# Low weights that are loaded as stationary operands, 32 bytes off the 128-byte phase of the other buffers

## The reference

```
x += 0.5 * SwiGLU_1(RMSNorm(x))                  # 1024 -> 2816 (gate and up) -> 1024
x += W_out [ DiffAttn | ConformerConv | ShortGatedConv ](W_in RMSNorm(x))
x += CrossAttn(RMSNorm(x), RMSNorm(mem))         # 4 heads of 256, 256 memory tokens
x += 0.5 * SwiGLU_2(RMSNorm(x))
```

## Time and profile before

| | |
|---|---|
| three runs, median | 1149.59 us |
| the same, lowest | 1149.45 us |
| the profiled execution's own time | 1149.58 us |
| its span, first to last instruction | 1147.8 us |
| mean granted TensorE clock | 1.00 of 2.4 GHz |
| PE busy | 1140.2 us, 99% of the span |
| DVE busy, ACT busy | 851.1 us (74%), 653.4 us (57%) |

### The profile page before, as it was taken

One profiled execution on the slowest core, in us unless ns is written; L12 is line 12 of the kernel. 1 busy time (PEld: TensorE's weight loads), 2 busy tenths in 40 slices (PEclk: granted clock), 3 DMA queues, 4 the chain that ended last, 5 costly groups with the idle time before them and its releaser, 6 DMA issues.

```text
span 1147.8 us, 15676 instructions
## 1 busy us (share of the span) xinstructions
PE 1140.2 (99%) x6180; PEld 985.8 (86%) x6180; DVE 851.1 (74%) x1164; ACT 653.4 (57%) x937; POOL 21.6 (2%) x63
## 2 busy tenths in 40 slices
PE   9999999999999999999999999999999999999997
PEld 8888888888889888888888888888888888888886
DVE  7767667899967676666786676669998676766756
ACT  6555556547755564545565554565577556645444
POOL 1000000000000000000000000000000000000000
PEclk9999999999999999999999999999999999999999
DMA  8865645644444366555546655544545443656551
GB/s 284 316 207 171 206 157 180 220 148 170 166 167 158 113 224 204 181 190 195 191 152 244 202 183 193 193 162 168 184 147 209 158 147 128 220 175 208 173 191 61
DMA packets 66265, 210.92 MB, mean 184 GB/s; under 512 B 5008, under 2 KB 24208, under 8 KB 61072
## 3 DMA queue, kind: packets, MB, share of 16 engines
q1 hardware_dynamic: 65216, 209.26, 53.6%
q10 hardware_dynamic: 976, 0.66, 0.2%
HBM read 208.85 MB, written 1.05 MB: 183 GB/s over the span
## 4 chain that ended last, share of the span: by engine, by line
PE 95%; DVE 4%; DVEq 1%; issue 0%; ACT 0%
PE G L1663 28%; PE G L1667 15%; PE D L1531 10%; PE D L1532 10%; PE D L1533 10%; PE G L1624 3%; PE D L1624 3%; PE G L1531 3%; PE G L1533 3%; PE G L1532 3%; PE G L1630 2%; DVE w_lo L974 1%; PE D L1630 1%; DVE acc L1181 1%; PE D L1598 1%; DVEq L1183 1%
## 5 line engine op out<-in xcount | busy, mean ns | idle before, releaser
L974 DVE TENSOR_TENSOR w_lo<-w_raw,w_hi 128x2048 fp32r<-128x2048 f32 (+3 forms) x260 | 452.2, 1746 | 54.8 <-ACT w_hi L563 53.8
L563 ACT ACTIVATE w_hi<-w_raw 128x2048 fp32r<-128x2048 f32 (+3 forms) x260 | 381.6, 1476 | 39.5 <-PE D L1533 16.9
L1663 PE MATMUL G<-a,w_hi 128*128 128x512 f32 x1406 | 339.7, 390 | 0.0
L1663 PEld LDWEIGHTS G<-a,w_hi 128*128 128x128 f32 x1406 | 260.8, 188 | 52.7 <-issue 0.9
L1667 PEld LDWEIGHTS G<-a,w_lo 128*128 128x128 f32 x1406 | 184.2, 191 | 9.5
L1667 PE MATMUL G<-a,w_lo 128*128 128x256 f32 x1406 | 187.0, 282 | 0.0
L1078 DVE TENSOR_TENSOR zqk<-G,zqk 128x512 f32<-128x512 f32 x88 | 60.7, 690 | 153.5 <-ACT zqk L642 153.2
L642 ACT ACTIVATE zqk<-G 128x512 f32<-128x512 f32 x88 | 52.4, 595 | 180.8 <-PE G L1667 180.5
L1531 PE MATMUL D<-w_hi,hT_hi 128*128 128x512 f32 x352 | 138.2, 393 | 0.0
L1532 PE MATMUL D<-w_lo,hT_hi 128*128 128x512 f32 x352 | 137.9, 392 | 0.0
L1533 PE MATMUL D<-w_hi,hT_lo 128*128 128x512 f32 x352 | 137.0, 389 | 0.0
(11 more groups left out here) (261 smaller groups left out, 1270.1 us busy)
## 6 DMA issues: line engine op xcount, KB each, us to landing
w_raw<-w_dram SPq DMA_DIRECT2D x120, 1024.0 KB, 5.0
w_raw<-w_dram SPq DMA_DIRECT2D x143, 512.0 KB, 5.4
m_raw<-memT_dram SPq DMA_DIRECT2D x2, 1024.0 KB, 9.4
w_raw<-w_dram SPq DMA_DIRECT2D x6, 256.0 KB, 5.8
w_raw<-w_dram SPq DMA_DIRECT2D x8, 128.0 KB, 4.0
vx<-mem_dram SPq DMA_DIRECT2D x1, 1024.0 KB, 10.7
x<-x_dram SPq DMA_DIRECT2D x2, 256.0 KB, 4.9
gbc<-fin_dram SPq DMA_DIRECT2D x1, 512.0 KB, 7.6
```

The costliest lines, as they stand in the source:

```text
L563: A(w_hi[:, part(i)], w_raw[:, part(i)], ACT.Copy).then_inc(s_hi, 1)
L974: V.tensor_tensor(w_lo[:, part(i)], w_raw[:, part(i)], w_hi[:, part(i)].bitcast(F32), ALU.subtract).then_inc(s_lo, 1)
L1663: M(banks[b], whi[:, at:at + P], both, start=k == 0, stop=False)
```

## The change

`w_lo` gets 192 more columns, and each block a place of its own in it, `PLACE_LO`. A block's columns are moved on by 32 columns (128 bytes) for each 1024 columns that lie before it, which leaves its phase, and the blocks whose low part is stationary in products of 256 columns by 8 columns (32 bytes) more. These are the 107 `gu` blocks of the feed-forward parts, the queries' 12 blocks, the 8 blocks of the memory's keys, and blocks 6, 7 and 8 of `in`, 133 of the 261. (In block 6 of `in` the low part moves; the change gives it the 32 bytes too.) All other blocks keep phase 0. `w_raw` and `w_hi` stay as they are. The buffers behind `w_lo` move on by 768 bytes, a multiple of 128, so their phase stays.

No instruction is added, removed or moved on any engine: each engine's list is that of before, row by row, apart from line numbers (31 more near the end of the file) and from the addresses that it reads and writes.

```
+LINE = 32
+SHIFT = 8
+GROUP = 1024
+RING_LO = RING + LINE * (RING // GROUP)
+
+def lo_is_stationary(name):
+
+    stage, piece = name[1], name[2]
+    if stage in ("ffn1", "ffn2"):
+        return piece[0] == "gu"
+    return stage == "q" or (stage == "kv" and piece < 4) or (stage == "in" and piece in (6, 7, 8))
+
+def lo_places():
+
+    place = []
+    for i, (name, w) in enumerate(RING_BLOCKS):
+        place.append(PLACE[i] + LINE * (PLACE[i] // GROUP) + (SHIFT if lo_is_stationary(name) else 0))
...
-        w_lo = sb("w_lo", [P, RING], F32R)
+        w_lo = sb("w_lo", [P, RING_LO], F32R)
...
+        def part_lo(i):
+
+            return slice(PLACE_LO[i], PLACE_LO[i] + RING_BLOCKS[i][1])
...
-                V.tensor_tensor(w_lo[:, part(i)], w_raw[:, part(i)], w_hi[:, part(i)].bitcast(F32), ALU.subtract
+                V.tensor_tensor(w_lo[:, part_lo(i)], w_raw[:, part(i)], w_hi[:, part(i)].bitcast(F32), ALU.subtract
...
-                return w_hi[:, part(i)], w_lo[:, part(i)]
+                return w_hi[:, part(i)], w_lo[:, part_lo(i)]
```

More of the change, by code:

```diff
@@ L102 @@
 PLACE, BEFORE = ring_places()
+LINE = 32
[11 more added lines that the diff above has]
+        place.append(PLACE[i] + LINE * (PLACE[i] // GROUP) + (SHIFT if lo_is_stationary(name) else 0))
+        for j in range(i):
+            apart = PLACE[j] + RING_BLOCKS[j][1] <= PLACE[i] or PLACE[i] + w <= PLACE[j]
+            assert not apart or place[j] + RING_BLOCKS[j][1] <= place[i] or place[i] + w <= place[j]
+    return place
+PLACE_LO = lo_places()
 TRANSFERS = [2 if (name[1] == "q" and name[2] >= 4) or (name[1] == "in" and name[2] in (7, 8)) or (
@@ L1014, in first_norm @@
                 dve.drain()
-                V.tensor_tensor(w_lo[:, part(0)], w_raw[:, part(0)], w_hi[:, part(0)].bitcast(F32), ALU.subtract
+                V.tensor_tensor(w_lo[:, part_lo(0)], w_raw[:, part(0)], w_hi[:, part(0)].bitcast(F32), ALU.subtract
                                 ).then_inc(s_lo, 1)
@@ L1671, in first_gate_up @@
             def first_gate_up():
-                whi, wlo = w_hi[:, part(0)], w_lo[:, part(0)]
+                whi, wlo = w_hi[:, part(0)], w_lo[:, part_lo(0)]
                 pe.wait_ge(s_first_w, 1)
```

## The result

The changed kernel takes **1152.79 us** (median of 9 runs, 1152.37 to 1153.27) against 1149.59 us before. The ratio is 1.0028 with a 95% interval of 1.0018 to 1.0039: slower by 0.3%, 3.2 us, where 0.45% faster was forecast, and outside the range of 1138.8 to 1150.4. Both forecast and result lie within the 2% about which the prediction gives 0.98.

The account below looks back on a forecast made before the run. PE's own steps were taken to bound the kernel. The only counted term, 5.2 us from 1726 low products at 3 ns each, gave 1149.6 - 5.2 = 1144.4 us, 0.45% faster; range 1138.8 to 1150.4.

Parts of the forecast that it names:

- What bounds the kernel: Whole kernel: PE is busy 1140.2 of 1147.8 us and waits 1.3 us, so the time is the sum of PE's steps.
- DVE's writes off phase: The 260 subtractions of line 974 write 32 bytes further on; cost nothing, since even a tenth more leaves DVE below PE.
- The larger margins of DVE and ACT: In a feed-forward piece of 8.28 us, DVE has 2.8 us and ACT 4.1 us to spare.
- The shifted low parts, stationary: 1726 products of lines 1667 and 1630 that load shifted low weights gain 3 ns each, 5.2 us.
- Products of 512 columns ... 226 ns each stays: Products loading `w_hi` keep their phase and 226 ns step; only the step from last 256 to first 512 may change.
- inside the uncertainty of the 3 ns: Step from the last 256 to the first 512, one for sixteen products: may change by a few ns, not counted separately.
- The buffers behind: Buffers after `w_lo` move by 768 bytes; cost nothing, with the reserve that a multiple of 256 is not shown.
- Nothing happens: Rival: the lost 13 ns is a fixed cost of changing weights, or another address period counts; 1149.6 us, chance 0.2.
- Slower: Rival: loads off the 128-byte line touch five lines instead of four, delaying the weight swap; 1150.2 to 1155 us, chance 0.08.
- The shortest step that a weight load of 128 columns shows anywhere: Transposes at 107.5 ns a step, bounding the low products' gain at 12.5 ns each, 21.6 us.
- A larger gain: Rival: parting two colliding read streams removes most of the loss; half gives 10.8 us, 1138.8 us; mostly 1134 to 1141, chance 0.17.

Follow-up runs that it names:

- with 256 bytes inserted: Changed kernel with 256 instead of 128 bytes inserted for each 1024 columns, shift still 32 bytes; 1150.33 us, ratio 1.0006 against the kernel before.
- the run with 224 bytes: Changed kernel with 256 instead of 128 bytes inserted for each 1024 columns and a shift of 224 instead of 32 bytes; 1146.33 us, ratio 0.9971.

## Why the prediction was wrong

**What bounds the kernel** was right. PE hardly waits in either kernel (1.3 and 1.6 us), and 74 pieces at 37 ns carry 2.8 of the 3.1 us that its steps lost. DVE's writes off phase cost nothing, as said: 850.9 us against 851.1. The larger margins of DVE and ACT were not touched.

**The term that failed first is "The shifted low parts, stationary"**, 3 ns a product and 5.2 us. In the changed kernel a low product in the pieces gained (1912.5 - 1905.1) / 16 = 0.5 ns, which makes 0.8 us of the 5.2 if all 1726 did, and with 256 bytes inserted 1.3 ns. I had two rows, the scores with 3.3 ns and the values with a loss of 0.9, noted that the values had "exactly the relation that the change makes", and then took a value near the scores as the longer undisturbed run. The scores load 32 bytes behind, not ahead. Their relation was made in the run with 224 bytes and gave the scores' step, 116.6 ns. With the change's direction, 32 ahead, it is 118.2. Neither is the values' 120.9: two thirds of the values load 32 ahead and one third 64 ahead, the last of their eleven steps took 0.13 us, and over all 96 values the median step of each line is 118 to 120 ns. Reading the durations as steps misled too: 188 ns for the loads and 280 for the products stand in the runs of 32, 96 and 224 bytes alike, while their steps differ by 1.6 ns.

**The second is "Products of 512 columns ... 226 ns each stays"**, and within it the step between the two widths, which was called "inside the uncertainty of the 3 ns". The edge that cost was the other one. The prediction spoke of the step from the last 256 to the first 512, which stayed (120.0 ns before, 120.5 in the changed kernel, 116.7 with 256 inserted); it had no term for the step from the last 512 to the first 256, 8.4 ns once a piece at 32 bytes, nor for the down products behind, which are slow to settle. Together they lose 28 ns a piece around the low products, more than the 21 that these gained. In the changed kernel the sum over a piece is 18.5 ns lost in the high products, 26.1 in the down products and 7.4 gained in the low ones. So the shift alone, with 256 bytes inserted, costs 0.7 us (1150.33 - 1149.60), which its interval does not tell from nothing.

**The third is that phase was taken modulo 128 bytes.** "The buffers behind" had the reserve that an offset of 256 bytes modulo 512 was not shown; that was harmless (1149.74 us). The harmful offset was in the ring itself, where the change adds 128 bytes a group "which leaves its phase". I took this as given and asked of no row whether 128 was the period; "Nothing happens" named another period and priced it at zero. The inserted bytes cost 2.3 us alone and 2.5 us beside the shift, most of the 3.2 us that the change lost. They act in two ways. Low parts that move lie off, in products which I had not listed as touched: 16.5 of the 30 ns a piece that the inserted bytes cost beside the shift are in the high and down products. And 672 loads lie 160 bytes ahead where 32 was meant: 13.5 ns a piece are in the low ones.

**The rivals.** "Slower" had the sign, and the time lies in its span of 1150.2 to 1155, but its mechanism is not the cause: loads 64, 96 and 224 bytes ahead start off the 128-byte line just as those 32 ahead do, and these kernels are the three fastest. "Nothing happens" missed the time, and the sentence of the Trainium skill behind it ("TensorE: Matmul & The Clock Gate", "Step-by-step: what each phase is for"), that a load takes nothing from the running product, is not borne out here as a rule for time: loads 96 bytes ahead in the down products cost 7.5 us with the same instructions. "The shortest step that a weight load of 128 columns shows anywhere" was not that: ahead of the values, four transposes of line 1925 take 357.53 to 357.88 us, three steps of 108 ns and one of 28 to the product behind. The bound fed "A larger gain" alone. "A larger gain" was right in that the parted streams can give more than the change gave, and its size, 10.8 us, was not reached at any of six offsets. The upper end of the range, 1150.4, allowed nothing for products of 512 columns, and that is where the loss was.

**What stays open** is the mechanism inside the chip. The runs show that steps depend on the address modulo 256 of what is loaded, what moves, and what moved just before, and that steady runs repeat fixed patterns. Whether two reads meet in one part of the memory was not tried directly. Nor was it parted whether moved low parts at another address cost because the streams that follow each other differ, or because each differs from the load beside it.

## What to carry to other kernels

When PE is the bound and never waits, the place of its operands modulo 256 bytes is a setting like any other, with 0.3% to gain and 1% to lose here from an unchanged list of instructions; whoever adds a buffer or pads a ring here should keep that address for all that PE moves. Take the step from start times, place by place in a run and over its edges, since durations hide it, and since what a run of products gains can be lost in the first steps of the next. A neighbour in the trace is evidence only with the direction, the width and the order in which it stands.

## What the runs showed of the hardware that was not expected

- At 512 float32r columns, equal addresses modulo 256 give the shortest steady step of the three relations tried, 226.7 ns at a granted clock of 1.00. A load 32 bytes behind the moving stream gives 233.6, one 96 ahead 229 to 238.
- At 256 columns the steady step is 120.0 ns with equal addresses and, on average, with loads 128 and 160 bytes ahead. Over a run of sixteen, its first step included, these three give 119.5, 120.3 and 120.0, and 224, 96, 64 and 32 bytes ahead give 116.6, 117.3, 117.9 and 118.2.
- Low parts that move at 0 among high ones at 128 modulo 256 cost 12.7 ns for each low one, with all loads of low parts at 0 as well, 2.3 us / 172 = 13 ns with 672 of the 1728 loads there. With a shift of 96 the count gives 7 ns (1.2 us / 172), but this holds the gain of the low products; the high and down products of a piece lose 18 ns there, against 20 without a shift.
- A run of equal phase takes up to nine products to reach its steady step, and the steps on the way lie between 3 ns below and 9 ns above it. In the down products of equal phase they end in the same steps, 236, 228, 232.5, 231, then 226.7 ns, or in the last of these, whichever run stands ahead.
